# Delta-rule solve on 64x64 diagonal blocks, and the samples' output projection in four column strips

## The reference, cut to what matters

```python
def step(S, inp):
    r_t, w_t, k_t, v_t, a_t, b_t = inp
    sa = jnp.einsum('bhij,bhj->bhi', S, a_t)
    S = S * w_t[:, :, None, :] + sa[..., None] * b_t[:, :, None, :] + v_t[..., None] * k_t[:, :, None, :]
    return S, jnp.einsum('bhij,bhj->bhi', S, r_t)
...
merged = (gate_a * o_ret + gate_b * o_rwkv).astype(xn.dtype)
return merged @ p['w_out'], ...
```

## Time and profile before

| what | us |
|---|---|
| median of three runs (lowest, highest) | 935.5 (934.65, 936.99) |
| the profiled execution | 933.9 |
| its span, from the first to the last instruction | 932.3 |
| one pass of the mixer loop | 66.1 |
| from 554 us in the last pass to the expert phase | 98.4 |
| expert phase | 279.9 |

### The profile page before, as it was taken

The page is one execution under the profiler, slowest core; times in us unless marked ns, Lnnn a source line. Parts: engine busy times, 40 slices in busy tenths (PEclk is TensorE's granted clock), DMA queues, the critical chain, the costliest instruction groups (busy, mean ns, idle before and its releaser), DMA issues. The chain is left out here.

```text
span 932.3 us, 13436 instructions
## 1 busy us (share of the span) xinstructions
PE 806.9 (87%) x5047; PEld 573.3 (61%) x5047; DVE 429.8 (46%) x994; ACT 219.1 (23%) x445; POOL 73.9 (8%) x71
## 2 busy tenths in 40 slices
PE   3689999999999999999999998937677788777984
PEld 2467887877977878878878876511653344324421
DVE  3153556547547546546555565782421232123224
ACT  3132505405314324324235041001100000000002
POOL 0000000000000000000000008950000000000000
PEclk9899999999999999999999999978589898889887
DMA  9834224224124224233242140110899999999961
GB/s 285 250 98 138 84 69 117 67 67 139 49 65 138 72 85 116 69 94 90 67 119 87 67 171 9 70 72 23 338 414 416 417 420 416 416 415 419 418 271 47
DMA packets 112603, 167.49 MB, mean 180 GB/s; under 512 B 7633, under 2 KB 91691, under 8 KB 103996
## 3 DMA queue, kind: packets, MB, share of 16 engines
q1 hardware_dynamic: 108876, 158.96, 47.3%
q0 software_dynamic: 1664, 4.98, 1.8%
q10 hardware_dynamic: 2032, 3.13, 1.0%
HBM read 158.63 MB, written 8.43 MB: 179 GB/s over the span
## 5 line engine op out<-in xcount | busy, mean ns | idle before, releaser
L275 PE MATMUL bank<-room,wall 128*128 128x264 f32 (+1 forms) x1152 | 287.2, 395 | 11.2 <-PEq L140 7.2
L275 PEld LDWEIGHTS bank<-room,wall 128*128 128x128 f32 x1152 | 212.3, 192 | 57.0 <-issue 15.3
L1553 PE MATMUL bank<-ring,xg 128*32 128x512 f32 x512 | 72.7, 732 | 35.5 <-DMA ring<-in_expert_w_up_dram 34.5
L1553 PEld LDWEIGHTS bank<-ring,xg 128*32 128x32 f32 x512 | 20.4, 132 | 87.0 <-issue 87.0
L1529 PEld LDWEIGHTS bank<-G,xn 128*128 128x128 f32 x384 | 44.9, 197 | 9.6 <-issue 5.9
L1529 PE MATMUL bank<-G,xn 128*128 128x128 f32 x384 | 46.4, 283 | 3.6 <-DVE GW L1777 3.6
L1805 DVE SCALAR_TENSOR_TENSOR th<-th,bank 128x256 f32<-128x256 f32 x8 | 3.4, 421 | 97.1 <-ACT th L1651 97.1
L1590 PE MATMUL bank<-y,GT 128*128 128x512 f32 x96 | 45.8, 612 | 1.0 <-issue 0.9
L275 PE MATMUL bank<-wall,merged 128*128 128x512 f32 (+1 forms) x96 | 44.4, 613 | 2.5 <-DVE merged L1314 2.5
L1794 DVE TENSOR_TENSOR x<-x,bank 128x512 f32<-128x512 f32 (+1 forms) x48 | 32.8, 684 | 12.2 <-PE bank L1590 12.2
L1112 POOL DMA_DIRECT2D out_rwkv_p_dram<-zout x8 | 4.9, 616 | 397.3 <-ACT zout L836 396.6
(11 more groups left out here) (366 smaller groups left out, 1316.4 us busy)
## 6 DMA issues: line engine op xcount, KB each, us to landing
wall<-in_w_in_dram SPq DMA_DIRECT2D x72, 512.0 KB, 3.6
ring<-in_expert_w_gate_dram SPq DMA_DIRECT2D x32, 1024.0 KB, 17.6
ring<-in_expert_w_up_dram SPq DMA_DIRECT2D x32, 1024.0 KB, 18.6
ring<-in_expert_w_down_dram SPq DMA_DIRECT2D x32, 1024.0 KB, 22.8
room<-in_state_ret_dram SPq DMA_DIRECT2D x8, 512.0 KB, 4.8
out_ret_s_dram<-room POOLq DMA_DIRECT2D x8, 512.0 KB, 3.8
wall<-in_w_out_dram SPq DMA_DIRECT2D x8, 512.0 KB, 3.5
room<-in_state_rwkv_dram SPq DMA_DIRECT2D x1, 2048.0 KB, 8.6
```

The lines of the kernel that those rows point to most:

```text
L275: return nc.tensor.matmul(out, lhsT, rhs, start=start, stop=stop, skip_group_check=loose)
L1553: last = mm(MB[e * CAP:(e + 1) * CAP, :], xg[:, b, kk, e * CAP:(e + 1) * CAP], w, start=(kk == 0), stop=(kk == KT - 1))
```

## The change

Nothing off the diagonal is stored or multiplied any more. The matrices of a unit are 128x64: the rows of the first chunk's block stand on partitions 0 to 63, those of the second on 64 to 127. Each former 128x128 product is two of 64x64, rows and columns 0 to 63 of the array for the first chunk and 64 to 127 for the second. Units are numbered with the head first (u = 2h + t). The products, Q and Y use all four quarters of the array, rows by head and columns by chunk or the other way round; Q and Y then stand in two banks each, one a chunk (`qbank`, `ybank`), so their evictions become two instructions, and the state chain waits once for the Y parts (`y_part`). The mask products become two instructions each instead of four, W1 and the copy of A4's transpose one instead of two. The samples' projection is cut in four strips of 256 columns, each on 32 columns of the array, into four partition ranges of bank 4, and the addition to `x` follows it with four instructions. The diff, cut to its core:

```diff
     m = np.zeros((P, 4, C))
+    m[:, 0] = (s // 16 == t // 16) & (s < t)
...
-        pr = xroom[:, 0:16 * P].rearrange("p (u n c) -> p u n c", u=4, n=4)
-        la = xroom[:, 16 * P:24 * P].rearrange("p (u n c) -> p u n c", u=4, n=2)
+        pr = xroom[:, 0:16 * C].rearrange("p (u n c) -> p u n c", u=4, n=4)
+        la = xroom[:, 16 * C:24 * C].rearrange("p (u n c) -> p u n c", u=4, n=2)
...
+        def v64(x):
+            return x[:, 0:4 * C].rearrange("p (u c) -> p u c", u=4)
+
+        UNITS = [(h, t, TT * h + t) for t in range(TT) for h in range(2)]
+        CHUNKS = [slice(0, C), slice(C, P)]
+        qbank, ybank = (M[2], M[0]), (M[3], M[1])
...
                 for t in range(TT):
+                    for m, src in enumerate((bt, kt)):
+                        for h in range(2):
+                            for ps in CHUNKS:
+                                hs = slice(HD * h, HD * h + HD)
+                                at = (2 * t + m) * P
+                                last = mm(pe, M[h][ps, at:at + P], src[hs, t * P + ps.start:t * P + ps.stop], ar[hs, t, :, ps], True, True)
+                last.then_inc(sem("prod"), 1)
+                for t in range(TT):
                     for h in range(2):
-                        u = 2 * t + h
-                        hs = slice(HD * h, HD * h + HD)
-                        cols = slice(t * P, (t + 1) * P)
-                        mm(pe, M[u][:, 0:2 * P], bt[hs, cols], ar[hs, t].rearrange("p a b -> p (a b)"), True, True)
-                        mm(pe, M[u][:, 2 * P:4 * P], kt[hs, cols], ar[hs, t].rearrange("p a b -> p (a b)"), True, True).then_inc(sem("prod"), 1)
-                for h in range(2):
-                    past(pe, f"tok_copy{h}", n)
-                    for t in range(TT):
-                        hs = slice(HD * h, HD * h + HD)
-                        last = mm(pe, M[4 + h][:, t * P:(t + 1) * P], ar[hs, t, 0, :], bt[hs, t * P:(t + 1) * P], True, True)
-                    last.then_inc(sem("prod"), 1)
+                        for ps in CHUNKS:
+                            hs = slice(HD * h, HD * h + HD)
+                            last = mm(pe, M[2 + h][ps, t * C:(t + 1) * C], ar[hs, t, 0, ps], bt[hs, t * P + ps.start:t * P + ps.stop], True, True)
+                last.then_inc(sem("prod"), 1)
...
                 for u in range(4):
-                    last = mm(pe, v4(M[0])[:, u, :], pr[:, u, 0, :], la[:, u, 0, :], True, True)
+                    for ps in CHUNKS:
+                        last = mm(pe, v64(M[0])[ps, u, :], pr[ps, u, 0, :], la[ps, u, 0, :], True, True)
                 last.then_inc(sem("a2_mm"), 1)
...
             def horner(src, bank, ready):
+                settle(pe)
                 past(pe, ready, n)
                 for u in range(4):
-                    last = mm(pe, v4(bank)[:, u, :], nt[:, u, :], src[:, u, :], True, True)
+                    for ps in CHUNKS:
+                        last = mm(pe, v4(bank)[ps, u, :], nt[ps, u, :], src[ps, u, :], True, True)
                 last.then_inc(sem("horner_mm"), 1)
...
-                for u in range(4):
-                    h, t = u % 2, u // 2
-                    hs = slice(HD * h, HD * h + HD)
-                    last = mm(pe, M[2][hs, t * P:(t + 1) * P], zf[:, u, 0:HD], pr[:, u, 1, :], True, True, True)
+                for h, t, u in UNITS:
+                    for par, ps in enumerate(CHUNKS):
+                        hs = slice(HD * h, HD * h + HD)
+                        last = mm(pe, qbank[par][hs, t * C:(t + 1) * C], zf[ps, u, 0:HD], pr[ps, u, 1, :], True, True, True)
                 last.then_inc(sem("q_mm"), 1)
...
+                for t in range(TT):
+                    for m in range(2):
+                        for h in range(2):
+                            for par, ps in enumerate(CHUNKS):
+                                u, hs = TT * h + t, slice(HD * h, HD * h + HD)
+                                lhsT, kind = (zf[ps, u, HD:P], 1) if m == 0 else (tmk[ps, t, 2, hs], 3)
+                                last = mm(pe, ybank[par][hs, t * C:(t + 1) * C], lhsT, pr[ps, u, kind, :], t == 0 and m == 0, False, True)
+                last.then_inc(sem("y_part"), 1)
...
+                    if c == 1:
+                        settle(pe)
+                        past(pe, "y_part", n)
...
-                for u in range(4):
-                    dve.wait_ge(sem("prod"), n * 6 + (u - 5))
-                    last = V.tensor_tensor(pr[:, u], v4(M[u]), mk[:], mult)
+                dve.wait_ge(sem("prod"), n * 2 - 1)
+                for h in range(2):
+                    last = V.tensor_tensor(pr[:, TT * h:TT * h + TT].rearrange("p t k c -> p t (k c)"), M[h][:].rearrange("p (t x) -> p t x", t=TT),
+                                           mk[:].rearrange("p k c -> p (k c)").unsqueeze(1).broadcast_to([P, TT, 4 * C]), mult)
                 last.then_inc(sem("masked"), 1)
...
+        def w_out_samples(pe):
+
+            for kk_ in range(KT):
+                for j in range(4):
+                    mm(pe, psum[4][32 * j:32 * j + B, 0:D // 4], merged[:, kk_, TP:T], wall[:, kk_, j * (D // 4):(j + 1) * (D // 4)],
+                       kk_ == 0, kk_ == KT - 1, True)
...
             pe.wait_ge(sem("merged_all"), 1)
-            w_out_part(pe, 2, range(KT))
+            w_out_samples(pe)
...
-                for hf in range(2):
-                    hc = slice(hf * 512, (hf + 1) * 512)
-                    last = V.tensor_tensor(x[0:B, 2, hc], x[0:B, 2, hc], psum[4 + hf][0:B, :], add)
+                for j in range(4):
+                    jc = slice(j * (D // 4), (j + 1) * (D // 4))
+                    last = V.tensor_tensor(x[0:B, 2, jc], x[0:B, 2, jc], psum[4][32 * j:32 * j + B, 0:D // 4], add)
```

More of the change, by code:

```diff
@@ L87, in constants @@
     s, t = np.meshgrid(np.arange(P), np.arange(P), indexing="ij")
[L88 to L94, removed]
+    s_, t_ = s, t
+    s, t = np.arange(P)[:, None] % C, np.arange(C)[None, :]
+    m = np.zeros((P, 4, C))
+    m[:, 0] = (s // 16 == t // 16) & (s < t)
+    m[:, 1] = s <= t
+    m[:, 2] = s < t
+    m[:, 3] = s <= t
     out["mk"] = m
-    lo = np.zeros((P, 2, P))
-    lo[:, 0] = same16 & (t < s)
-    lo[:, 1] = same64 & ~same16 & (t < s)
+    lo = np.zeros((P, 2, C))
+    lo[:, 0] = (s // 16 == t // 16) & (t < s)
+    lo[:, 1] = (s // 16 != t // 16) & (t < s)
     out["mlo"] = lo
     out["ident"] = np.eye(P)
-    out["one64"] = (s // HD == t // HD).astype(np.float64)
+    out["one64"] = (s_ // HD == t_ // HD).astype(np.float64)
     out["mean64"] = out["one64"] / HD
@@ L108, in constants @@
     out["scanm"] = sm
-    out["tri"] = (s < t).astype(np.float64)
+    out["tri"] = (s_ < t_).astype(np.float64)
     out["ones"] = np.ones((P, P))
@@ L604, in pe_pass @@
                 for u in range(4):
-                    last = mm(pe, v4(M[5])[:, u, :], at4w[:, u, 0, :], a4[:, u, :], True, True)
+                    for ps in CHUNKS:
+                        last = mm(pe, v64(M[5])[ps, u, :], at4w[ps, u, 0, :], a4[ps, u, :], True, True)
                 last.then_inc(sem("a8_mm"), 1)
                 for u in range(4):
-                    last = mm(pe, v4(M[1])[:, u, :], a4[:, u, :], at4w[:, u, 1, :], True, True)
+                    for ps in CHUNKS:
+                        last = mm(pe, v64(M[1])[ps, u, :], a4[ps, u, :], at4w[ps, u, 1, :], True, True)
                 last.then_inc(sem("w2_mm"), 1)
@@ L620, in pe_pass @@
                 for u in range(4):
-                    last = mm(pe, v4(M[2])[:, u, :], a8[:, u, :], w2s[:, u, :], True, True)
+                    for ps in CHUNKS:
+                        last = mm(pe, v64(M[2])[ps, u, :], a8[ps, u, :], w2s[ps, u, :], True, True)
                 last.then_inc(sem("w3_mm"), 1)
@@ L798, in act_pass @@
                 past(act, "a2_mm", n)
-                A.copy(a2[:], v4(M[0])).then_inc(sem("a2_copy"), 1)
+                A.copy(a2, v64(M[0])).then_inc(sem("a2_copy"), 1)
                 past(act, "lakv_mm", n)
-                A.copy(rhs[:, :, 1, :], M[4][:, 0:4 * HD].rearrange("p (u c) -> p u c", u=4)).then_inc(sem("rhs_ready"), 1)
+                A.copy(rhs[:, :, 1, :], v64(M[4])).then_inc(sem("rhs_ready"), 1)
                 past(act, "at4w1_mm", n)
-                for half in range(2):
-                    last = A.copy(at4w[:, 2 * half:2 * half + 2, 0, :], M[2 + half][:].rearrange("p (u a c) -> p u a c", u=2, a=2)[:, :, 0, :])
-                last.then_inc(sem("at4_copy"), 1)
+                A.copy(at4w[:, :, 0, :], M[2][:].rearrange("p (u a c) -> p u a c", u=4, a=2)[:, :, 0, :]).then_inc(sem("at4_copy"), 1)
                 past(act, "a4_mm", n)
-                A.copy(a4[:], v4(M[0])).then_inc(sem("a4_copy"), 1)
+                A.copy(a4, v64(M[0])).then_inc(sem("a4_copy"), 1)
             if front:
@@ L832, in act_pass @@
                 past(act, "y_mm", n)
-                A.copy(ys[:, 0:TP], M[3][:, 0:TP]).then_inc(sem("y_copy"), 1)
```

(12 more changed lines are left out.)

87 lines of the change are left out of this document (45 added, 42 removed).

## The result

The change took the kernel from 935.6 us (934.65 to 936.99) to **899.08 us** (897.24 to 900.09, four runs of each), a ratio of 0.9606 (95% interval 0.9587 to 0.9626; brackets behind a ratio below are such intervals). The forecast was 901.0 with a range of 889 to 913. The profiled execution took 899.27 us, its span 897.6.

A forecast was written before the change was run, and what follows sets the result against it. TensorE was taken to bound the mixer loop. Seven passes at -2.92 us (-20.4), the last pass -3.6 and the samples' projection -10.3 sum to -34.3 us: 901 us, range 889 to 913.

The forecast's parts named there:

- Quarters side by side: Solve blocks: two diagonal quarter passes run together, 0.028 us average per 64-column pass; squares with LAKV -0.92 us.
- Rival 2: Diagonal quarters take turns in their common PSUM bank: a loop pass 5.2 us longer, 966 us in all; 4%.
- Four quarters at once: Products and LA over all four array quarters: 1.12 us plus about 0.15 for an extra change of shape.
- Rival 1: Only two quarters run at once: -1.39 us a loop pass instead of -2.92, 912 us in all; 20%.
- The excursions: Leaving the whole array and coming back costs 0.35 us each; the three Horner steps lose 1.05 us a pass.
- Rival 4: Changes of shape cost less, 0.15 us, in longer blocks: 11 us more gain, 890 us in all; 10%.
- Q, F/G and Y: Loop blocks: Q and Y become 48 quarter passes over four quarters, an excursion before and after; -0.66 us a pass.
- Third Horner step: Loop: operand stays 128 columns wide, so quarters win nothing and the excursion adds 0.35 us.
- The table load: Loop front: ScalarE's table load lets the tanh start only 0.75 us earlier, so products and LA gain 0.75 us.
- rival 3: The loop is held by the evictions and gains nothing, only the tail counts: 922 us; 6%.
- The last pass: Tail: the solve finishes earlier until GpSimd's end on the sample state bounds it; -3.6 us, range 0 to -3.7.
- The samples' projection: Mixer end: 64 passes of 256 columns in four strips, half of them at half clock; 15.62 to 5.3 us, -10.3.

The follow-up runs named there:

- chunk_outer: The changed kernel with all of the first chunk's quarter products before the second's in each diagonal block of the solve, instead of alternating; 925.59 us.
- horner_full: The changed kernel with the three Horner steps on the whole array again, N's transpose kept as a zero-padded 128x128 block diagonal; 894.02 us.
- tok_late: The changed kernel with ScalarE's copies of the token rows moved behind the two tanh; 897.78 us.
- gp_less: The changed kernel without GpSimd's second slice of the sample state, a quarter of the samples' state and output; 887.44 us.
- strips_off: The changed kernel with the samples' projection as before (16 matmuls of 512 columns), the solve as changed; 908.6 us.

## Why the prediction was right, and where its terms were not

**Quarters side by side: as forecast.** Squares with LAKV take 355.05 - 353.51 = 1.54 us where 1.71 was expected and 2.7 would have meant taking turns; A4 with W1 1.49 where 1.69 was. Rival 2 (966 us) falls, and chunk_outer shows that the overlap is what the gain hangs on: with a part of it gone its pass is 3.70 us longer (taking turns was priced at 8.1), though the work, the banks and the shapes are the same. The rule that the forecast quoted from the Trainium skill ("TensorEngine Tiling (Array Packing)", "Restrictions and Gotchas") is not what these runs show: two row tiles wrote one bank on different partitions with starts 0.006 us apart.

**Four quarters at once: as forecast.** The 32 passes of the products take 347.85 - 346.93 = 0.92 us, 0.029 each, and LA's 16 another 0.34: 1.26 us, forecast 1.12 + 0.15. Rival 1 (912 us) wanted 2.2.

**The excursions: as forecast.** The first two Horner steps cost 0.32 and 0.30 more, against 0.35, and horner_full took 0.78 off the pass for the three, where the table has 0.75 and the forecast 1.05. Only the place was different: a Horner block itself lasts 1.02 us, not 1.24, and the rest stands in the projection behind it (371.18 to 373.15 is 1.97 where it was 1.78). The five blocks before the Horner steps, each with one excursion priced at 0.35, came out within 0.02 of their forecasts. Rival 4 (890 us, excursions at 0.15) falls.

**Two terms of the loop were mis-sized**, and they are the 0.5 us by which a pass is better than the forecast.
- *Q, F/G and Y: -0.97, not -0.66.* The step "both take an excursion before and after" failed. Before, the block went from the whole array to 128x64 for Q, to 64x64 for F/G, back to 128x64 for Y and back: by the prices of the forecast, 24 passes at 0.056, 48 at 0.028 and two excursions of 0.35 make 3.39, the 3.36 seen. After, everything is 64x64: 48 at 0.014, 48 at 0.028 and one excursion make 2.37, and 381.50 - 379.10 = 2.40 is seen. Counted that way the term would have come out right. That is worked out from rows; no kernel tested it by itself.
- *Third Horner step: +0.13, not +0.35.* Before, the block lasted 392.19 - 391.20 = 0.99 us instead of 0.89, and the half V projection behind it 394.07 - 392.19 = 1.88 instead of 1.78. The second 0.1 fits the change to 128x64 that came next; where the first is from no row says. Neither is there after. This too is from the rows alone.

**The table load: as forecast, a little low.** TensorE idles 0.56 us there, forecast about 0.7, and the block gives -0.64 where -0.75 was expected; tok_late took the load out of the way and won 0.18. Up to the start of the R projection the gain is what was forecast, 3.45 - 2.71 = 0.74; the other 0.1 is in that projection, which lasts 3.87 us instead of 3.77 now that quarters follow it.

**No new wait in the loop.** Between block and projection TensorE idles nowhere else, so rival 3 (922 us) falls. What was costed at nothing cost nothing.

**The last pass: -1.45, not -3.6.** The solve did its part. The loop moved GpSimd's start by 23.2 us; the last pass's solve starts 563.22 - 538.57 = 24.65 earlier, 1.45 beyond that (forecast 1.9), and its results reach VectorE 27.04 us earlier, 3.84 beyond (forecast 3.9). The step that failed is "GpSimd is late next", with GpSimd's end as the only bound. VectorE met GpSimd sooner: from the `yc` row to its last instruction it took 623.13 - 596.10 = 27.03 us before and 598.48 - 569.06 = 29.42 after, for the same instructions. All of the 2.39 lies in products that ran beside GpSimd both times: which engine waits for the other fell out differently. The first went from 1.23 to 2.08 us; before, the GpSimd row beside it was the long one (3.21 us at 596.67, where the same step takes 2.35 at 573.69 after). Why the turns fell as they did no run shows. That gave 2.39 of the 3.84 back. So the transfer left when VectorE was through, as before, and not at GpSimd's end (597.31); GpSimd itself took 1.1 us longer from first to last (59.3, before 58.2). gp_less shows the link: with part of GpSimd's work gone, the same VectorE work ends 9.3 us earlier.

**The samples' projection: -10.4, forecast -10.3.** 5.19 us against 5.3; strips_off gave it back. The mechanism is the forecast's: the first half of the 64 passes takes 3.27 us at a granted clock of 0.51 (forecast 3.5), the rest 1.92 at 1.00 (forecast 1.8). Over the six profiles with strips read for it the projection takes 5.06 to 5.65 us. (One pass of 512 columns alone is 0.44 us by the forecast's own working, not 0.43; no term hangs on it.)

Sum by what was measured: -23.2 up to GpSimd's start (forecast -20.4), -1.45 (-3.6), -10.4 (-10.3) and +0.4 elsewhere, -34.7 against -34.3. That the total is nearer than its terms is luck: the errors had opposite signs.

## What to carry to other kernels

Cut block-diagonal products into array quarters where it shortens the moving operand or fills four quarters; where the right side keeps its width the excursion (about 0.3 us here) is a pure loss, and a zero-padded whole-array product is faster. Let the quarters alternate in program order: in another order they overlapped only in part. And before crediting a stage with time, see which engine works beside the one that ends it: here GpSimd held the tail back although VectorE ended it.

## What the runs showed that was not expected

In the two blocks read, a quarter that stands later in the order begins about four passes ahead of its turn, not more: eight passes in a row for each quarter took 1.51 us where alternating took 1.02. Part of an excursion's cost shows in the matmuls after it (1.97 instead of 1.78 us), not in the block that made it. And VectorE's products of two SBUF operands can wait for a whole GpSimd instruction: its 128x256 product of 576.35 ends at 578.36, 0.28 us behind the GpSimd row that began at 576.12 and ended at 578.08; the next, of 578.39, ends at 580.85, 0.28 behind GpSimd's 580.57. Each takes 0.42 when GpSimd has ended. It goes the other way too, as GpSimd's 3.21 us at 596.67 shows. A reduction in the same stretch, with one operand, takes its 1.22 us beside GpSimd as without it. The Trainium skill ("SBUF — State Buffer", "Who interferes with whom") says that a VectorE product with both inputs in SBUF contends with GpSimd's reads and that a reduction never does; these rows agree with both.
